# One state per 128 rows in a gated linear-attention scan, with the scores between its blocks taken from the block borders

## What is computed

```
def _gla_chunked(q, k, v, log_a):          # GLA_CHUNK = 16
    acs = jnp.cumsum(log_a.reshape(n, nc, c, h, dk), axis=2)
    seg = acs[:, :, :, None] - acs[:, :, None, :]
    decay = jnp.exp(jnp.where(tril, seg, -jnp.inf))
    scores = jnp.einsum('ncihd,ncjhd,ncijhd->nchij', q, k, decay)
    o_intra = jnp.einsum('nchij,ncjhv->ncihv', scores, v)
    q_dec = q * jnp.exp(acs)
    k_dec = k * jnp.exp(acs[:, :, -1:] - acs)
    states = jnp.einsum('ncjhd,ncjhv->nchdv', k_dec, v)
    chunk_decay = jnp.exp(acs[:, :, -1])
    ...  # scan over chunks: S = S * chunk_decay + states
    o_inter = jnp.einsum('ncihd,nchdv->ncihv', q_dec, s_in)
    return (o_intra + o_inter)
```

## Time and profile before

| | |
|---|---|
| median of 3 runs | 3356.75 us (3344.27 to 3367.16) |
| profiled execution | 3348.65 us, span 3346.5 us |
| busy shares over the span | PE 89%, DVE 56%, ACT 34% |
| the stage, first gate matmul to the last state of SSD | 297.0 to 635.7 us, 338.7 us |
| in it | PE busy 236.65, DVE 194.07, ACT 34.81 us; granted clock 0.76 |

### The profile page before, as it was taken

The page is one execution under the profiler, slowest core; times in us unless marked ns, Lnnn a source line. Parts: engine busy times, 40 slices in busy tenths (PEclk is TensorE's granted clock), DMA queues, the critical chain, the costliest instruction groups (busy, mean ns, idle before and its releaser), DMA issues.

```text
span 3346.5 us, 42308 instructions
## 1 busy us (share of the span) xinstructions
PE 2984.3 (89%) x16998; PEld 2243.3 (67%) x16998; DVE 1889.5 (56%) x3457; ACT 1121.6 (34%) x2018; POOL 150.5 (4%) x139
## 2 busy tenths in 40 slices
PE   8996676788877999999998898779999997799998
PEld 4886555567744666766664576468888775578887
DVE  4256645544556677777764768753233478643333
ACT  3322000221211455555553232642222333632222
POOL 0000000000000122221220000000000000000000
PEclk9998777789988999999999998889999998899999
DMA  5210000022122598899997521031423220031321
GB/s 207 100 34 21 0 0 0 1 78 83 47 99 101 196 348 343 348 354 354 353 352 284 221 84 49 1 104 56 131 76 104 86 76 32 11 116 60 123 70 69
DMA packets 179070, 432.39 MB, mean 129 GB/s; under 512 B 19586, under 2 KB 107939, under 8 KB 159540
## 3 DMA queue, kind: packets, MB, share of 16 engines
q1 hardware_dynamic: 160148, 396.02, 32.9%
q0 software_dynamic: 18720, 33.60, 2.7%
HBM read 425.87 MB, written 38.29 MB: 139 GB/s over the span
## 4 chain that ended last, share of the span: by engine, by line
PE 63%; DVE 10%; DMA 4%; ACT 2%; issue 2%; POOL 0%; SPq 0%; POOLq 0%; DVEq 0%
PE ps L280 14%; PE ps L281 13%; PE ps L282 13%; PE ps L2303 5%; DMA ring<-in_ew 2%; PE ps L1669 2%; PE ps L1380 2%; PE ps L1839 2%; PE ps L2329 1%; DMA hg<-h_rows,idx 1%; DVE Pb L3210 1%; PE ps L2542 1%; PE ps L2942 1%; PE ps L2026 1%; DVE bi L3043 1%
## 5 line engine op out<-in xcount | busy, mean ns | idle before, releaser
L2742 DVE TENSOR_TENSOR wf<-ring,wf 128x1024 fp32r<-128x1024 f32 (+1 forms) x152 | 181.6, 1197 | 336.1 <-ACT wf L2738 336.1
L280 PE MATMUL ps<-hxh,wf 128*128 128x512 f32 x704 | 276.0, 392 | 2.8 <-DVE hxl L2887 2.8
L281 PE MATMUL ps<-hxl,wf 128*128 128x512 f32 x704 | 275.4, 391 | 0.0
L282 PE MATMUL ps<-hxh,wf 128*128 128x512 f32 x704 | 275.3, 391 | 0.0
L2738 ACT ACTIVATE wf<-ring 128x1024 fp32r<-128x1024 f32 (+1 forms) x152 | 156.5, 1032 | 352.8 <-PE ps L282 352.8
L2241 DVE TENSOR_TENSOR spA<-ring,spA 128x1024 fp32r<-128x1024 f32 x156 | 184.3, 1221 | 102.1 <-ACT spA L2236 101.9
L2303 PE MATMUL ps<-ring,hdT 128*128 128x512 f32 x520 | 234.8, 594 | 0.8 <-issue 0.8
L2236 ACT ACTIVATE spA<-ring 128x1024 fp32r<-128x1024 f32 x156 | 157.4, 1053 | 57.5 <-DMA ring<-in_ew 51.3
L2241 DVE TENSOR_TENSOR spB<-ring,spB 128x1024 fp32r<-128x1024 f32 x104 | 124.0, 1221 | 70.1 <-ACT spB L2236 70.1
L2303 PEld LDWEIGHTS ps<-ring,hdT 128*128 128x128 f32 x520 | 93.8, 190 | 94.3 <-issue 90.9
L280 PEld LDWEIGHTS ps<-hxh,wf 128*128 128x128 f32 x704 | 133.2, 189 | 31.4 <-DVE hxl L2887 3.6
(11 more groups left out here) (581 smaller groups left out, 6572.3 us busy)
## 6 DMA issues: line engine op xcount, KB each, us to landing
ring<-in_ew SPq DMA_DIRECT2D x65, 2048.0 KB, 12.4
ring<-in_ew SPq DMA_DIRECT2D x65, 1024.0 KB, 6.7
ring<-in_w_in SPq DMA_DIRECT2D x17, 2048.0 KB, 7.8
ring<-in_w_gate SPq DMA_DIRECT2D x20, 1024.0 KB, 5.4
ring<-in_w_up SPq DMA_DIRECT2D x20, 1024.0 KB, 8.0
ring<-in_w_down SPq DMA_DIRECT2D x16, 1024.0 KB, 5.0
ring<-in_w_out SPq DMA_DIRECT2D x6, 2048.0 KB, 7.9
yr<-y_rows SPq DMA_DIRECT2D x12, 1024.0 KB, 10.9
```

The source lines that it names most:

```text
L280: pe.matmul(o, lhs[0], rhs[0], start=start, stop=False)
L281: pe.matmul(o, lhs[0], rhs[1], start=False, stop=False)
L282: return pe.matmul(o, lhs[1], rhs[0], start=False, stop=stop)
L2742: v.tensor_tensor(item_part(n)[1], item_raw(n), f(item_part(n)[0]), ALU.subtract).then_inc(*w_lo.inc(n))
```

## The change

One GLA block has now one state for its 128 rows instead of eight: one product of keys and values, one mask, one update. The output takes the state once. The scores inside 16-row blocks are computed as before, but for the four heads in one matmul: the queries stand in a buffer `qbd` of four 128-row slots, zero outside their head's 32 rows, so that one 512-column matmul over 128 rows does the four heads. The scores between blocks come from three more levels: halves of 64 within 128, of 32 within 64, of 16 within 32. For each level the decays run from the border between the two halves, whose sums come from a table `lvl` that is loaded in `again_sp`; the matmuls of the lower levels give 64 and 32 rows of output. One DVE addition brings both kinds of scores together. An x block has 14 steps now and a context block 6, so GLA has 68 rounds, as SSD has, and the norm of the GLA result stands behind them.

The new part of the diff; the removed code of the three GLA functions is what is printed above:

```diff
+def _level_mats():
+    ...
+        for w in (64, 32, 16):
+            query = (t // w) % 2 == 1 - d
+            out.append((s // w == t // w) & np.where(query, le, gt))
@@ again_sp, setup_dve
+        sp.dma_start(lvl, A["lvl"]).then_inc(*d_lvl.inc("in"))
...
+        v.memset(qbd, 0.0).then_inc(*V.inc())
+        v.wait_ge(*V.val())
+        v.wait_ge(*b_evA.val(("gq", 0)))
+        for h in range(4):
+            v.tensor_copy(qbd[32 * h:32 * h + 32, h, :], gqT[32 * h:32 * h + 32, :]).then_inc(*V.inc())
         for d in range(2):
-            v.memset(GB[d]["qx"], 0.0).then_inc(*V.inc())
-            i = v.memset(Sg[:, d, 0, :], 0.0)
-            i.then_inc(*(c_las.inc("zero") if d else V.inc()))
+            v.memset(GB[d]["xk"], 0.0).then_inc(*V.inc())
+            v.memset(GB[d]["xq64"], 0.0).then_inc(*V.inc())
+            v.memset(GB[d]["S"][:, 0, :], 0.0).then_inc(*(c_las.inc("zero") if d else V.inc()))
@@ gla_pe
+            if x:
+                pe.matmul(gb[:, 0:384], la, lvl[:, 384 * d:384 * d + 384])
+                pe.matmul(ga[:, 0:256], la, sums)
+            pe.matmul(ga[:, 256:384], C(f"g128_{d}"), la)
+            pe.matmul(ga[:, 384:385], la, C("ones")[:, 0:1]).then_inc(*G.inc((u, "cum")))
+            yield from rest(4 if x else 3)
             if x:
                 pe.wait_ge(*Gd.val((u, "qp")))
+                pe.matmul(gb[:, :], kp, xqd).then_inc(*G.inc((u, "sc")))
+                yield from rest(2)
+                pe.wait_ge(*Gd.val((u, "xq")))
+                pe.matmul(ga4, xk[:, 0, :], B["xq64"], start=True, stop=False)
+                for b in range(2):
+                    at = 64 * b + 32 * (1 - d)
+                    pe.matmul(ga4[64 * b:64 * b + 64, :, at:at + 32], xk[:, 1, 64 * b:64 * b + 64], B["xq32"][:, :, b, :], start=False, stop=False)
+                for b in range(4):
+                    at = 32 * b + 16 * (1 - d)
+                    m = pe.matmul(ga4[32 * b:32 * b + 32, :, at:at + 16], xk[:, 2, 32 * b:32 * b + 32], B["xq16"][:, :, b, :],
+                                  start=False, stop=True)
+                m.then_inc(*G.inc((u, "cr")))
+                yield from rest(2)
+            if i < 5:
+                ...
+                pe.matmul(gb[:, 0:256], B["eq"][:, 384:512], gkv[:, b6, 128:384]).then_inc(*G.inc((u, "kv")))
+            yield from rest(2)
             if x:
+                pe.wait_ge(*Gd.val((u, "sa")))
+                pe.matmul(ga[:, 0:256], qx, B["S"][:, i % 2, :], start=True, stop=False)
                 for h in range(4):
                     m = pe.matmul(ga[:, 64 * h:64 * h + 64], sTg[:, h * 128:(h + 1) * 128], gkv[:, b6, 128 + 64 * h:192 + 64 * h],
                                   start=False, stop=(h == 3))
                 m.then_inc(*G.inc((u, "out")))
+                yield from rest(3)
@@ gla_act
+            yield
...
             if x:
+                act.wait_ge(*G.val((u, "cum")))
+                act.activation(B["el"], gb[:, 0:384].rearrange("p (l t) -> p l t", l=3), ACT.Exp, scale=1.0 / 16).then_inc(*Ga.inc((u, "el")))
+                act.wait_ge(*Gd.val((u, "cq")))
+                act.activation(eq[:, 0:128], cq, ACT.Exp, scale=1.0 / 16)
+                act.activation(eq[:, 128:256], cq, ACT.Exp, scale=-1.0 / 16).then_inc(*Ga.inc((u, "q")))
+                act.activation(eq[:, 256:512], ga[:, 128:384], ACT.Exp, scale=1.0 / 16)
...
+            act.activation(etot[:, 0:1], ga[:, 384:385], ACT.Exp, scale=1.0 / 16).then_inc(*Ga.inc((u, "e")))
+            yield from rest(13 if x else 5)
@@ gla_dve
+            yield from rest(2)
             v.wait_ge(*Ga.val((u, "e")))
+            v.tensor_tensor(eq[:, 384:512], eq[:, 384:512], gkv[:, b6, 0:128], ALU.mult).then_inc(*Gd.inc((u, "kd")))
             if x:
+                v.tensor_tensor(B["kp"], gkT[:, tok], eq[:, 128:256], ALU.mult)
+                v.tensor_tensor(B["xqd"], qbd[:, :, xt_], bcm(eq[:, 0:128], 4), ALU.mult).then_inc(*Gd.inc((u, "qp")))
+                yield from rest(2)
+                for l, w in enumerate((64, 32, 16)):
+                    v.tensor_tensor(half(xk[:, l, :], w, True), half(gkT[:, tok], w, True), half(el[:, l, :], w, True), ALU.mult)
+                for l, w in enumerate((64, 32, 16)):
+                    ...
+                m.then_inc(*Gd.inc((u, "xq")))
+                v.tensor_tensor(B["qx"], gqT[:, xt_], eq[:, 256:384], ALU.mult).then_inc(*Gd.inc((u, "qx")))
+                yield from rest(2)
                 v.wait_ge(*G.val((u, "sc")))
                 v.tensor_tensor(v4(sTg), v4(gb[:, :]), bcm(C(f"i16_{d}"), 4), ALU.mult).then_inc(*Gd.inc((u, "s")))
+                v.wait_ge(*Gd.val((u, "s")))
                 yield
+                v.wait_ge(*G.val((u, "cr")))
+                v.tensor_tensor(sTg, sTg, ga[:, :], ALU.add).then_inc(*Gd.inc((u, "sa")))
+            yield from rest(2)
+            if i < 5:
+                v.wait_ge(*G.val((u, "kv")))
+                v.tensor_tensor(stm, gb[:, 0:256], C("bd"), ALU.mult).then_inc(*Gd.inc((u, "m")))
+                ...
+                v.scalar_tensor_tensor(out=S_[:, (i + 1) % 2, :], in0=S_[:, i % 2, :], scalar=etot[:, 0:1], in1=stm, op0=ALU.mult,
+                                       op1=ALU.add).then_inc(*Gd.inc((u, "S")))
+            yield from rest(2)
             if x:
                 ...
+                yield from rest(3)
```

More of the change, by code:

```diff
@@ L27, in _const_mats @@
         b16 = s // 16 == t // 16
+        half = (s % 16 < 8) if d == 0 else (s % 16 >= 8)
+        m[f"q16_{d}"] = (le & (s // 16 == t // 16)).astype(np.float32) - (half & (s // 16 == t // 16))
         m[f"i128_{d}"] = le
@@ L69, in _const_mats @@
     return out, np.ascontiguousarray(np.concatenate(parts, 1))
+def _level_mats():
+    i = np.arange(128)
+    s, t = i[:, None], i[None, :]
+    out = []
+    for d in range(2):
+        le = (s <= t) if d == 0 else (s >= t)
+        gt = (s > t) if d == 0 else (s < t)
+        for w in (64, 32, 16):
+            query = (t // w) % 2 == 1 - d
+            out.append((s // w == t // w) & np.where(query, le, gt))
+    return np.ascontiguousarray(np.concatenate(out, 1).astype(np.float32))
 def _rope_tables():
@@ L1028, in _program, with gla_keys, rest @@
     GU = [(i, d) for d in range(2) for i in range(6)]
-    g_pe = [Signal(sem(f"gla_mm{d}"), keys(GU[6 * d:6 * d + 6], "cum ~sc kv0 kv1 kv2 kv3 ~out")) for d in range(2)]
-    g_act = [Signal(sem(f"gla_scalar{d}"), keys(GU[6 * d:6 * d + 6], "e ~q")) for d in range(2)]
-    g_dve = [Signal(sem(f"gla_vector{d}"), keys(GU[6 * d:6 * d + 6], "~cq kd kde ~qp ~qx ~s m0 s0 m1 s1 m2 s2 m3 s3 ~o cp")) for d in range(2)]
+    GLA_PE = ("cum", "sc", "cr", "kv", "out")
+    GLA_DVE = ("cq", "kd", "qp", "xq", "qx", "s", "sa", "m", "S", "o")
+    def gla_keys(names, context, last):
+        return [[((i, d), k) for i in range(6) for k in names if (i >= 2 or k in context) and (i < 5 or k not in last)] for d in range(2)]
+    g_pe = [Signal(sem(f"gla_mm{d}"), k) for d, k in enumerate(gla_keys(GLA_PE, ("cum", "kv"), ("kv",)))]
+    g_act = [Signal(sem(f"gla_scalar{d}"), k) for d, k in enumerate(gla_keys(("el", "q", "e"), ("e",), ()))]
+    g_dve = [Signal(sem(f"gla_vector{d}"), k) for d, k in enumerate(gla_keys(GLA_DVE, ("kd", "m", "S"), ("m", "S")))]
+    def rest(n):
+        for _ in range(n):
+            yield
     def gla_pe(pe, d):
         B, ga, gb = GB[d], ps[4 + 2 * d], ps[5 + 2 * d]
-        kde, qx, sTg, S_ = B["kde"], B["qx"], B["sTg"], Sg[:, d, :, :]
-        qp = B["qp"].rearrange("p (a t) -> p a t", a=2)
+        kp, xqd, xk, qx, sTg = B["kp"], B["xqd"], B["xk"], B["qx"], B["sTg"]
+        ga4 = ga[:, :].rearrange("p (h t) -> p h t", h=4)
+        a = cmap[f"q16_{d}"][0]
+        sums = csb[:, a:a + 256]
         G, Ga, Gd = g_pe[d], g_act[d], g_dve[d]
@@ L1043, in gla_pe @@
                 pe.wait_ge(*c_las.val("zero"))
+                pe.wait_ge(*d_lvl.val("in"))
             else:
[L1045 to L1053, removed]
+                pe.wait_ge(*Gd.val(((i - 1, d), "o" if i > 2 else "m")))
@@ L1112, in gla_dve, with half @@
+            yield from rest(13 if x else 5)
     def gla_dve(v, d):
         B, ga, gb = GB[d], ps[4 + 2 * d], ps[5 + 2 * d]
-        kde, stm, qx, sTg, cq, etot = (B[n] for n in ("kde", "stm", "qx", "sTg", "cq", "etot"))
-        eq, qp, S_ = B["eq"].rearrange("p (a t) -> p a t", a=4), B["qp"].rearrange("p (a t) -> p a t", a=2), Sg[:, d, :, :]
+        cq, eq, etot, stm, S_, sTg, el, xk = (B[n] for n in ("cq", "eq", "etot", "stm", "S", "sTg", "el", "xk"))
         G, Ga, Gd = g_pe[d], g_act[d], g_dve[d]
+        def half(n, w, key):
+            z = n.rearrange("p (b c) -> p b c", c=2 * w)
+            first = key == (d == 0)
+            return z[:, :, 0:w] if first else z[:, :, w:2 * w]
@@ L1117, in gla_dve, with heads @@
+        def heads(w):
+            z = qbd[:, :, xt_].rearrange("p h (b c) -> p h b c", c=2 * w)
+            return z[:, :, :, 0:w] if d else z[:, :, :, w:2 * w]
```

112 lines of the change are left out of this document (38 added, 74 removed).

## The result

The changed kernel takes 3239.94 us (median of 4 runs, 3232.66 to 3240.61), the kernel before 3354.19 (4 runs): a ratio of 0.9652, 95% interval 0.9616 to 0.9689. Timed again later over 5 runs it was 0.9622 (0.9606 to 0.9639). The profiled execution took 3240.61 us, its span is 3238.5. The forecast was 3260, its range 3218 to 3306. The time is inside, but two steps behind the number were off in opposite directions: the stage gained 125.7 us, not 89, and 17.6 of these were gone by the end, as the two profiled executions show it (by the medians 114.3 us are left).

The account below looks back on a forecast made before the run. The hand-over between PE and DVE bounds the stage; context 28, four x blocks of 53 us and smaller terms end it at 546.3 instead of 635.7, so 3348.65 - 89 = 3260 us, range 3218 to 3306.

Parts of the forecast that it names:

- The floor of 32.2 us: Two SSD units, 14 rounds, of an x block: 16.1 us each, which this change cannot cut.
- Setup, context, norm: Around the x blocks: setup some 2 us later, context of 12 rounds 28 us, GLA norm standing alone 6.3 us.
- The x block: 14 rounds of both directions: 15 to 27 us on top of 32.2, so 53 us (47 to 59).
- Unit A: First SSD unit of an x block: added GLA work on the path 12.2 us, 20.8 at the low clock.
- unit B: Second SSD unit of an x block: additions, masks, states, output matmuls and copies add 3.0 us, 5.0 at the low clock.
- the clock's weight: In the x block: PE at 1.2 GHz for 0.48 of the stage, so 15 + 0.48 x 12 = 20.8 us added.
- the scores between blocks: Between SSD's output and its state product: 3.6 us on the path, 8.8 at the low clock.
- the second rival: PE never leaves 1.2 GHz: 64 us a block, 3304 us in all; chance 0.16.
- the fourth rival: Narrow matmuls cost 0.44 us a record like 32-row ones: 7.6 us a block, 3290 us in all; chance 0.08.
- So the gain reaches the end: Behind the scan stage: everything hangs on its end, so all 89 us gained there stay in the total.
- The slower rival: Rounds run one engine after another, nothing of GLA beside SSD: 82 us a block, 3388 us; chance 0.04.
- the first rival: PE stays at 2.4 GHz and the waits close: 44 us a block or less, 3224 us; chance 0.12.

Follow-up runs that it names:

- experiment 9: Changed kernel with GLA work left out of three x blocks and matmuls nobody reads added in their SSD units: 30.4 us a block.
- experiment 10: Changed kernel with GLA work moved into DVE's gaps, output earlier, line 1001 ahead of 995 and 998, bias over 128 rows: 3171.42 us, ratio to before 0.9449.
- experiment 6: Changed kernel with GLA's exponentials, kd, kp, xqd one round later and head scores behind the segment sums: 38.0 us a block.
- Experiments 2: Changed kernel with GLA work left out of three x blocks and the sum of directions left out, so SSD runs alone there: 34.5 us a block.
- experiment 4: Changed kernel with the next stage's bias matmul over 128 rows, 127 zeroed, instead of one row: 3231.76 us; the six pairs 10.6 us.

## Why the prediction was right, and where it was not

- **The bound and its removal: right.** Hand-over, not work, set the stage. Fewer operations in one block, and 14 rounds cost 44.4 us where 9 had cost 57.2. The floor of 32.2 us under it was not one: it came from a unit that ran at a clock of 0.79, and two units took 30.4 us in experiment 9 and 31.5 with all of GLA in experiment 10.
- **Setup, context, norm: right.** 1.5 for 2, 27.0 for 28, 5.25 for 6.3 us (the terms of the last add up to 6.15).
- **The x block: the size failed, 44.4 for 53,** outside the 47 to 59 of the forecast. Unit A takes 26.6 us in the mean of four (27.0, 26.4, 25.8, 27.2) and unit B 17.8 (18.9, 17.5, 18.1, 16.6), where 16.1 + 16.3 and 16.1 + 4.0 came out of the working, with the clock's weight. Most of the 8.6 us too many is the clock's weight: by it 15 us of added work became 20.8, and 12.2 were measured (44.4 - 32.2).
- **The term that was mis-sized is the scores between blocks.** The working has 3.6 us at the high clock, 8.8 at the low, 6.1 with the weight; in the trace line 1028 starts 2.2 us behind SSD's sums in the mean of the four. In the block shown, nearly all of it at the high clock, PE came from the end of 928 to the end of 937 in 4.45 us instead of 5.7, and DVE was ready after 2.9 us instead of 2.1. The working put 0.25 us on a narrow matmul of two records, from the 64-column row, so 1.5 on the six of a direction; in the trace the next matmul starts 0.62 us after the first of them. So a direction took 1.9 and 1.7 us, less than the 2.4 to 4.6 that the prediction looked for.
- **The other terms of unit A came out near their size at the high clock:** 2.0 us for the exponentials against a wait of 1.89, and 2.1 for kd, kp, xqd against 2.0 (both came back in experiment 6). The level factors and head scores part the two 1011 by 3.5 us in the mean, 0.7 in the bare unit of the earlier trace rows: 2.8 against 2.7. Line 995 starts 2.3 us behind the state in the mean, 0.7 in the bare unit: 1.6 against the 1.8 for the gate sums. There the working itself does not add up, since 3.3 less 2.1 us makes 1.2.
- **The clock: its level nearly right (0.80 for 0.75), its weight wrong.** I let 0.48 of the added PE work run at 1.2 GHz, as if the clock were given from outside. Experiments 2 and 9 show that the added work also raises it: 0.68 alone, 0.80 with GLA, 0.88 with idle matmuls. The rule of the Trainium skill that I weighed ("TensorE: Matmul & The Clock Gate", HAM oscillation), bursts that start each time at half clock, agrees with 919 in unit A (2.04 us for 8 records behind 5.89 us of idle time) and not with unit B (2.02 us for 16 behind 1.87 us of idle time); its upper end for all terms, the second rival with 64 us, did not come about.
- **The narrow matmuls: the fourth rival falls.** The drain at a change of tiling mode (the Trainium skill, "TensorEngine Tiling (Array Packing)", Key Properties) shows no cost with fewer output rows. With fewer contraction rows the trace agrees with it: 0.19 us more from start to start when matmuls over one row and over 128 alternate (experiment 4); that this is a drain is not shown.
- **"So the gain reaches the end": wrong by 17.6 us.** A later stage that grows was one of the prediction's own signs of being wrong, and one did grow. At the output stage 113.0 of 125.7 us were left (841.79 instead of 954.82). 7.2 went in the pairs; 2.5 behind them, where the clock stayed at 0.50 until 568 (from the first weights to the first product of the RWKV scan 11.8 for 9.4 us); 2.8 in that scan (271.2 for 268.4; the variants spread from 271.2 to 281.7, so this is not told from chance). The other 5 lie behind, where two executions of the same kernel differ by 10. The 7.2 us hang on the moment at which the clock fell: with the same pairs experiment 6 lost nothing there (13.6 us). The second failure hid half of the first: with the stage sized right the same sum says 3348.65 - 125.65 = 3223. That 3260 came within 20 us of the measured time is so far luck.

The slower rival (82 us a block) is refuted; the first rival had the block (44) and not the reason, since PE did not stay at 2.4 GHz.

What stays open: why the clock falls at another moment from one execution to the next, and with which edit of experiment 10 the last 2.5 us a block came.

## What to carry to other kernels

When strands share in-order engines, price an added operation by the gap it falls into, not by its length: look for what the next waiting instruction does meanwhile, as DVE's masks did here. Then move what stands ahead of a wait on the longest strand behind it; here that was worth 44 to 31.5 us a block with the same matmuls, part of it because TensorE, with shorter gaps, kept its high clock. And look at the first matmuls behind a stage that was shortened: a low clock there took back 9.7 of 125.7 us here, and matmuls over 128 rows, 127 of them zeros, kept it high.

## What the runs showed of the hardware

- TensorE's clock fell to 1.2 GHz among matmuls without a gap (in the changed kernel PE was busy for 17.88 of 17.90 us) in all eleven traces in which matmuls over one row alternate with full ones, the kernel before among them, 3.0 to 11.7 us after the first of them. In the two in which all ran over 128 rows it stayed at 2.4 GHz to their end and beyond (until 20.5 and 22.4 us after the first). In the 6 us ahead PE was busy for 4.6 us in all thirteen. What about the one-row matmuls does it, no run shows. The Trainium skill, "TensorE: Matmul & The Clock Gate", Part 1, lets the gate follow how busy PE has been; by the profile's busy time alone this fall is not explained.
- Six matmuls more in a block, whose result nobody reads, made it 4.1 us shorter (34.5 to 30.4), with the clock up from 0.68 to 0.88.
- Matmuls with 64 or 32 output rows follow full ones without a gap: eight records of 32 rows and 64 columns in 0.32 us.
